# Stick-breaking attention on Trainium2: value sums on unsplit fp32 operands, two heads in the two column halves of TensorE

## The chip, the cores and the metric
One core of one Trainium2 chip runs the whole program. The metric is the device time in microseconds (us) of one execution. TensorE (PE) multiplies, VectorE (DVE), ScalarE (ACT) and GpSimd (POOL) work element by element, SyncE (SP) issues the transfers.

## What is computed
Two transformer-like blocks on one sequence of 1024 rows and 1024 channels, in fp32. The first block is a short-convolution layer and a stick-breaking attention layer with 16 heads of 64; the second has pooling, differential attention and a feed-forward part. The change is in the attention of the first block:

```
z = q @ k.T / sqrt(64);  mask = kpos < qpos
log_beta = log_sigmoid(z);  log_1m_beta = where(mask, log_beta - z, 0)
suffix = reverse_cumsum(log_1m_beta) - log_1m_beta
a = where(mask, exp(log_beta + suffix), 0);  o = a @ v
x = x + gate * ((o * silu(zgate)) @ w_out)
```

## The kernel before
TensorE's fast way takes operands of a rounded fp32 type (F32R). To keep fp32 accuracy, an operand is split into a high part, rounded by ScalarE, and a low part, the remainder, formed by VectorE in `low` (its instruction stands at L1420) or by GpSimd. A product is then two or three matmuls. A matmul whose operands are plain F32 needs no split; the trace lists two instructions for each.

**The kv stage** makes keys and values for eight pairs of heads (`kv_chunks`, 16 chunks of 48 matmuls). The values of a pair are evicted to VST, turned by TensorE, and written to VS by ScalarE (`values_hi`, high part) and VectorE (`values_lo`, low part). High and low values of a head lie beside each other, 64 and 64 columns, so that one weight load of 128 columns holds both. VS goes to DRAM (1024 KB a pair) and comes back later in bV.

**The attention stage** (`attention_b`) has one round j for each pair of heads; round 0 stands ahead of a loop, six rounds run in the loop, and round 7 (`fill=False`) behind it. A round has eight steps t, one for each block of 128 queries. What each engine does in a step t:

- TensorE: `scores(t)` for both heads (head h in row half h of PE, into PSUM pair 1+h), then `turn(t-1, h)`, which transposes the weights of the step before, in groups of up to four blocks that alternate between two PSUM banks, then, if t is even, `values(t-1, h)`, the sums over the values for the 256 queries of blocks t-2 and t-1. Between them `steps(n)` places n of the 96 matmuls of the next round's query and gate projection (`B_FILL` says how many in which place: a, c, d, e).
- ScalarE: `weigh(t, h)` (two sigmoids, L1135 and L1136) and, between the heads, `turned(t-1, h)`, the eviction of a transposed group to ATH (L1128); at even t also `lower`, which copies 64 rows of each head's value sums (L1146).
- VectorE: `left(t, h)`, the running product along the keys (a scan, L1601), and behind each head's scan `turned(t-1, h)`, which forms ATL = PSUM - ATH (L1420, semaphore b_atl); at even t `outputs`, which adds the other 64 rows (L1610).
- GpSimd: the product of beta and the running product (L1882), and at odd t `gated`, the multiplication with the gate (L1873).

All of it is an order written out by hand. A scan waits for the second sigmoid of its head; `scores(t+1)` waits until both scans of step t have read PSUM (`free[1+h]`); `turn(t-1, h)` waits for GpSimd's product and for the ATL of the group two back, whose bank it takes; `values(t-1, h)` waits for the last ATL of its head. For each key block it issues two matmuls of 256 columns (128 at the diagonal block), one on ATH and one on ATL, with 128 weight columns, the high and low values of that head. Its 128 output rows are two halves that still have to be added, which `lower` and `outputs` do. Groups and counts are kept by `pair_group`. At odd t no value sums are made.

## Time and profile before

| | us |
|---|---|
| time, median of 3 runs (3079.27 to 3080.32) | 3079.79 |
| profiled execution | 3079.05 |
| its span | 3077.3 |
| PE busy | 2841.6 (92%) |
| DVE busy | 1271.5 (41%) |
| ACT busy | 1128.6 (37%) |
| POOL busy | 716.3 (23%) |

The attention stage of the first block lies from 725 to 1200 us. Its rounds in the loop take 58.9 us each: the scores of t=1 begin at 1020.76 us in one round and at 1079.63 us in the next. Busy is time with an instruction under way; a matmul's end is modelled, so PE's issue is read from the starts of successive rows. A time of the timeline is in us from the span's start. In a row, the bracket behind it is the idle time of the engine before it and what ended it. "PEclk" is the granted clock of TensorE as a share of full speed.

### The profile page before, as it was taken

To read this page: it belongs to the slowest core of one execution; us is meant where nothing else is said; L and a number is where in the kernel's file an instruction comes from. 1 tells how busy PE (TensorE), PEld (TensorE's weight loads), DVE (VectorE), ACT (ScalarE), POOL (GpSimd) and SP (SyncE) were. 2 spreads that over 40 slices of the span, in tenths; PEclk is the share of its full clock that TensorE was granted. 3 is DMA by queue.
4 is the path that set the end of the run, shared out by engine and by line. 5 is a ranking of instruction groups with operands and counts; after the bars stand their busy time and mean duration, and the time that the engine had idled before them with its cause. 6 is when DMAs were issued, how large, how long until landed. Compare 5 with 4: busy or idle time off the path is not lost.

```text
span 3077.3 us, 38234 instructions
## 1 busy us (share of the span) xinstructions
PE 2841.6 (92%) x13672; PEld 2282.4 (74%) x13672; DVE 1271.5 (41%) x1817; ACT 1128.6 (37%) x1586; POOL 716.3 (23%) x387
## 2 busy tenths in 40 slices
PE   5999998998888888798999999998898999999999
PEld 3888886886777777677876766765686888888887
DVE  5544433116666666370014655657433312112121
ACT  3222213225666554333125666665312212111120
POOL 0222221223444443112221111110121222222222
PEclk8999999998999998999999999999898999999999
DMA  5333320552121122112331001011421111111112
GB/s 196 128 123 116 130 70 33 186 181 84 49 89 55 48 82 87 44 41 96 116 119 35 28 28 34 35 34 48 149 91 41 48 48 48 48 48 48 47 54 97
DMA packets 62571, 236.82 MB, mean 77 GB/s; under 512 B 6944, under 2 KB 7584, under 8 KB 59936
## 3 DMA queue, kind: packets, MB, share of 16 engines
q1 hardware_dynamic: 62496, 235.88, 22.3%
q8 instruction: 40, 0.66, 0.1%
q14 instruction: 35, 0.29, 0.0%
HBM read 191.81 MB, written 44.04 MB: 77 GB/s over the span
## 4 chain that ended last, share of the span: by engine, by line
PE 47%; issue 38%; DVE 7%; POOL 4%; ACT 3%; DMA 0%; POOLq 0%; DVEq 0%; ACTq 0%; SPq 0%
PE PS L558 37%; POOL WL L1854 3%; DVE bC L1601 2%; DVE ATL L1420 2%; PE PS L718 2%; PE PS L740 2%; PE PS L674 2%; ACT PS L1136 1%; PE PS L905 1%; PE PS L768 1%; PE PS L886 1%; PE PS L703 1%; PE PS L723 0%; DMA TMP<-mods 0%; ACT ATH L1310 0%
## 5 line engine op out<-in xcount | busy, mean ns | idle before, releaser
L1854 POOL TENSOR_TENSOR WL<-WR,WH 128x1024 fp32r<-128x1024 f32 x215 | 518.2, 2410 | 2071.6 <-ACT WH L1004 1939.2
L558 PE MATMUL PS<-HH,WH 128*128 128x512 f32 x2256 | 715.7, 399 | 85.0 <-issue 29.9
L558 PE MATMUL PS<-HL,WH 128*128 128x512 f32 x2256 | 704.1, 394 | 0.0
L558 PE MATMUL PS<-HH,WL 128*128 128x512 f32 x2256 | 702.7, 393 | 0.0
L558 PEld LDWEIGHTS PS<-HH,WH 128*128 128x128 f32 x2256 | 421.7, 191 | 187.5 <-issue 65.7
L558 PEld LDWEIGHTS PS<-HL,WH 128*128 128x128 f32 x2256 | 429.3, 190 | 91.5
L558 PEld LDWEIGHTS PS<-HH,WL 128*128 128x128 f32 x2256 | 428.8, 190 | 91.3
L1004 ACT ACTIVATE WH<-WR 128x1024 fp32r<-128x1024 f32 x214 | 225.9, 1056 | 642.3 <-PE PS L558 462.9
L558 PE MATMUL PS<-GH,WH 128*128 128x512 f32 x768 | 236.6, 389 | 1.5 <-DVE TMP L1824 1.5
L558 PE MATMUL PS<-GL,WH 128*128 128x512 f32 x768 | 236.5, 389 | 0.0
L558 PE MATMUL PS<-GH,WL 128*128 128x512 f32 x768 | 236.4, 389 | 0.0
L1882 POOL TENSOR_TENSOR bB<-bB,bC 128x256 f32<-128x256 f32 (+7 forms) x128 | 154.2, 1207 | 276.7 <-DVE bC L1601 275.6
L1601 DVE TENSOR_TENSOR_SCAN bC<-PS,EPSC 128x256 f32<-128x256 f32 (+7 forms) x128 | 172.8, 1350 | 96.7 <-ACT PS L1136 96.3
L558 PEld LDWEIGHTS PS<-GH,WH 128*128 128x128 f32 x768 | 144.0, 188 | 32.1 <-issue 1.9
L558 PEld LDWEIGHTS PS<-GH,WL 128*128 128x128 f32 x768 | 144.2, 188 | 30.0
L558 PEld LDWEIGHTS PS<-GL,WH 128*128 128x128 f32 x768 | 144.2, 188 | 29.9
L1420 DVE TENSOR_TENSOR ATL<-PS,ATH 128x512 fp32r<-128x512 f32 (+3 forms) x288 | 151.3, 544 | 32.0 <-ACT ATH L1310 25.9
L1846 DVE TENSOR_TENSOR X<-PS,X 128x1024 f32 x32 | 39.2, 1225 | 292.2 <-PE PS L558 292.2
L1837 DVE SCALAR_TENSOR_TENSOR TMP<-PS,TMP 128x1024 f32<-128x1024 f32 x32 | 39.2, 1224 | 207.6 <-ACT TMP L1399 207.6
L703 PE MATMUL PS<-IDF,bB 128*128 128x128 f32 x576 | 93.7, 291 | 28.1 <-DVE ATL L1420 28.0
L1399 ACT ACTIVATE TMP<-PS 128x1024 f32<-128x1024 f32 x32 | 32.9, 1029 | 233.2 <-PE PS L558 233.2
L1479 DVE CUSTOM_DVE_ANT_0 TMP<-TMP,TMP 128x1024 f32<-128x1024 f32 x48 | 59.8, 1246 | 132.8 <-DMA TMP<-mods 131.5
(226 smaller groups left out, 3579.8 us busy)
## 6 DMA issues: line engine op xcount, KB each, us to landing
WR<-wst SPq DMA_DIRECT2D x215, 512.0 KB, 3.5
TMP<-mods SPq DMA_DIRECT2D x48, 512.0 KB, 3.6
MRAW<-mods SPq DMA_DIRECT2D x16, 512.0 KB, 10.7
v_hl<-VS SPq DMA_DIRECT2D x8, 1024.0 KB, 6.3
bV<-v_hl SPq DMA_DIRECT2D x8, 1024.0 KB, 7.8
X<-xt SPq DMA_DIRECT2D x4, 1024.0 KB, 8.0
x_b<-X SPq DMA_DIRECT2D x8, 512.0 KB, 4.8
k_hi<-KSH SPq DMA_DIRECT2D x8, 512.0 KB, 5.0
```

The source lines that it names most:

```text
L558: last = pe.matmul(PS[:, dst0 + q:dst0 + q + HALF], l, rr[:, k * S + q:k * S + q + HALF], start=a, stop=z)
L674: last = pe.matmul(PS[:, OB + (2 * n + r) * P:OB + (2 * n + 2) * P], v[:, kb * P:(kb + 1) * P], a[:, (2 * kb + r) * P:(2 * kb + 2) * P], s ...
L703: last = pe.transpose(PS[:, base + n * P:base + (n + 1) * P], bB[t % 2][h][:, kb * P:(kb + 1) * P], IDF[:, :])
L718: pe.matmul(PS[:, base + c0:base + c0 + w], l[par][rows, q], rr[par][rows, c0:c0 + w], start=i == 0, stop=i == 2 and c0 + w < n)
L740: last = pe.matmul(PS[:, o + r * P:o + 2 * P], value_weights(V, kb, h), a[:, (2 * kb + r) * P:(2 * kb + 2) * P], start=i == 0 and a is ATH ...
L1004: act.activation(WH[slot][:, :], WR0[:, :], ACT.Identity).then_inc(w_hi, 1)
L1420: return dve.tensor_tensor(dst, value, high.bitcast(F32), ALU.subtract)
L1479: dve.tensor_tensor_reduce(out=weights, in0=weights, in1=CB, scale=1.0, scalar=0.0, op0=ALU.mult, op1=ALU.add, accum_out=dst).then_inc(mod ...
L1601: dve.tensor_tensor_scan(bC[h][:, S - n:S][:, ::-1], c, EPSC[:, 0:1].broadcast_to([P, n]), 1.0, ALU.mult, ALU.bypass).then_inc(free[1 + h], 1)
L1837: dve.scalar_tensor_tensor(out=T[2 + m], in0=PAIR[s], scalar=0.0, in1=T[m], op0=ALU.max, op1=ALU.mult).then_inc(free[s], 1)
L1854: pool.tensor_tensor(WL[slot][:, :], WR0[:, :], WH[slot][:, :].bitcast(F32), ALU.subtract).then_inc(w_lo, 1)
L1882: pool.tensor_tensor(b, b, bC[h][:, S - n + 1:S + 1], ALU.mult).then_inc(b_a, 1)
```

## The change
The values are no longer split: VS and bV hold S columns of F32, ScalarE alone writes VS, and the store and the load are 512 KB. The transposed weights are not split either: ScalarE copies the groups of head 0, VectorE those of head 1, each into its own F32 tile of a double-buffered bAT, each with its own semaphore. `values(t)` handles both heads together: for each key block one F32 matmul a head, with 64 weight columns, head 0 into PSUM partitions 0 to 63 and head 1 into 64 to 127, of the same columns; it waits for both heads' groups. Value sums alternate between two halves of their bank. Their 128 rows are whole, so `lower` and the additions go, and `outputs` multiplies them with the gate on VectorE, straight from PSUM, in place of `gated` on GpSimd. In the last round the output of t=1 is gated in step 4 rather than 2.

```diff
@@ layout and names
-        VS = place("VS", 2 * S, F32R, r)
+        VS = place("VS", S, F32, r)
...
-        bOT = place("bOT", 2 * P, F32, r)
...
-        bV = [place(f"bV{i}", 2 * S, F32R, r) for i in range(2)]
+        bV = [place(f"bV{i}", S, F32, r) for i in range(2)]
...
+        bAT = [[nc.alloc_sbuf_tensor_at(f"bAT{i}{h}", [P, 2 * S], F32, offset=XAT + 8 * S * (2 * i + h)) for h in range(2)]
+               for i in range(2)]
...
         def value_weights(V, kb, h):
-            return V[:, (2 * kb + h) * P:(2 * kb + h + 1) * P]
+            return V[:, kb * P + h * HD:kb * P + (h + 1) * HD]
+        def value_bank(t):
+            o = OB + (t // 2) % 2 * 2 * P
+            return o, o + 2 * P
@@ SyncE: one 512 KB store and one 512 KB load of values a pair of heads
-                sp.dma_start(row(v_hl, i), VS[:, :].bitcast(F32)).then_inc(st_v, 16)
+                sp.dma_start(row(v_t, i), VS[:, :]).then_inc(st_v, 16)
@@ TensorE, turn(t, h)
-                        before = pair_group(t, h, g) - 1
-                        if not (first and before <= 0):
-                            pe.wait_ge(b_atl, NB * j + before)
+                        t0, h0, g0 = pair_group_two_back(t, h, g)
+                        if not (first and t0 < 0):
+                            pe.wait_ge(b_at[h0], NG * j + (group_index(t0) + g0 + 1))
@@ TensorE, values
-                def values(t, h):
+                def values(t):
                     if t < 0 and first:
                         return
-                    if not (first and t < 2):
-                        pe.wait_ge(b_os, ST * j + (t - 1))
-                    pe.wait_ge(b_atl, NB * j + pair_group(t, h, len(GROUP_BLOCKS[t % ST])))
+                    if not (first and t == 1):
+                        pe.wait_ge(b_o, ST // 2 * j + (t - 1) // 2)
+                    for h in range(2):
+                        pe.wait_ge(b_at[h], NG * j + group_index(t + 1))
                     V, t = bV[par if t >= 0 else 1 - par], t % ST
-                    o = OB + 2 * h * P
+                    o, end = value_bank(t)
                     for i, kb in enumerate((0, t, *range(1, t))):
                         r = 1 if kb == t else 0
-                        for a in (ATH[h], ATL[h]):
-                            last = pe.matmul(PS[:, o + r * P:o + 2 * P], value_weights(V, kb, h),
-                                             a[:, (2 * kb + r) * P:(2 * kb + 2) * P],
-                                             start=i == 0 and a is ATH[h], stop=i == t and a is ATL[h])
+                        for h in range(2):
+                            last = pe.matmul(PS[h * HD:(h + 1) * HD, o + r * P:end], value_weights(V, kb, h),
+                                             bAT[t // 2 % 2][h][:, (2 * kb + r) * P:(2 * kb + 2) * P],
+                                             start=i == 0, stop=i == t)
                     last.then_inc(b_av, 1)
...
                     if t % 2 == 0:
-                        values(t - 1, 0)
                         steps(d)
-                        values(t - 1, 1)
+                        values(t - 1)
@@ ScalarE: values of the kv stage in one copy; turned takes head 0 alone; lower is gone
-                act.activation(value_part(0), PAIR[2].rearrange("p (a d) -> p a d", d=HD), ACT.Identity).then_inc(kv_vh, 1)
+                act.activation(VS[:, :], PAIR[2], ACT.Identity).then_inc(free[2], 1)
...
-                def turned(t, h):
+                def turned(t):
...
-                    if t % 2 == 0 and not (first and t < 2):
-                        act.wait_ge(b_av, ST * j + (t - 1 + h))
+                    if t % 2 == 0 and not (first and t < 4):
+                        act.wait_ge(b_av, ST // 2 * j + (t // 2 - 1))
...
-                        act.wait_ge(b_t, NB * j + (pair_group(t, h, g) + 1))
-                        act.activation(at_blocks(ATH[h], t % 2, bl[0], bl[-1] + 1),
-                                       turned_blocks(len(bl), turn_bank(t, h, g)), ACT.Identity).then_inc(b_ath, 1)
+                        act.wait_ge(b_t, NB * j + (pair_group(t, 0, g) + 1))
+                        act.activation(at_blocks(bAT[t // 2 % 2][0], t % 2, bl[0], bl[-1] + 1),
+                                       turned_blocks(len(bl), turn_bank(t, 0, g)), ACT.Identity).then_inc(b_at[0], 1)
@@ VectorE: values_lo is gone; turned copies head 1; outputs gates
-                        dve.wait_ge(b_ath, NB * j + (pair_group(t, h, g) + 1))
-                        b = (t % 2, bl[0], bl[-1] + 1)
-                        low(at_blocks(ATL[h], *b), turned_blocks(len(bl), turn_bank(t, h, g)),
-                            at_blocks(ATH[h], *b)).then_inc(b_atl, 1)
+                        dve.wait_ge(b_t, NB * j + (pair_group(t, 1, g) + 1))
+                        dve.tensor_copy(at_blocks(bAT[t // 2 % 2][1], t % 2, bl[0], bl[-1] + 1),
+                                        turned_blocks(len(bl), turn_bank(t, 1, g))).then_inc(b_at[1], 1)
...
+                def outputs(t):
...
+                    b = slice((t % ST - 1) * P, (t % ST + 1) * P)
+                    o, end = value_bank(t % ST)
+                    y = bZS[par if t >= 0 else 1 - par][:, b]
+                    if t == 1 or t == 5:
+                        dve.wait_ge(b_df, 4 * j + (1 if t == 1 else 2))
+                    dve.wait_ge(b_av, ST // 2 * j + (t + 1) // 2)
+                    dve.tensor_tensor(y, PS[:, o:end], y, ALU.mult).then_inc(b_o, 1)
...
                 for t in range(ST):
                     left(t, 0)
-                    turned(t - 1, 0)
                     left(t, 1)
-                    turned(t - 1, 1)
+                    turned(t - 1)
                     if t in halves:
                         evict(halves[t])
                     if not fill and t == ST - 1:
                         operand_lo("y", 0, bZS)
-                    if t % 2 == 0:
-                        outputs(t - 1, 0)
-                        outputs(t - 1, 1)
+                    if not fill and t == 4:
+                        outputs(1)
+                    if t % 2 == 0 and (fill or t != 2):
+                        outputs(t - 1)
@@ GpSimd: gated is gone
-                    if t % 2 == 1:
-                        gated(t - 2)
```

`pair_group_two_back(t, h, g)` gives the step, head and group that stand two places ahead in the order of groups. The staging tiles of the output projection move by one place, since bV is smaller.

## Rows read from the trace of the kernel before

**Rows 1.** Windows: length, busy us of PE, PEld, DVE, ACT, POOL; clock, DMA.
```profile
902.00:961.00 59.00, 52.28 (x355) 42.53 (x355) 37.79 (x52) 35.43 (x70) 26.64 (x22) 1.00 0.18 62
1138.00:1200.00 62.00, 46.82 (x292) 39.03 (x292) 39.23 (x50) 35.63 (x67) 26.82 (x20) 0.83 0.16 57
```

**Rows 2.** Waits in two middle rounds: us in total, times, longest us.
```profile
PE PS L718 <- DVE bC L1601: 5.3, 8, 1.2
PE PS L703 <- DVE ATL L1420: 5.0, 4, 1.3
PE PS L740 <- DVE ATL L1420: 3.0, 6, 0.7
```

**Rows 3.** Groups by line, two middle rounds: count, busy us, mean ns.
```profile
L1420 DVE TENSOR_TENSOR ATL<-PS,ATH 128x512 fp32r<-128x512 f32 (+3 forms) x48 | 24.5, 539 | 1.1 <-ACT ATH L1128 0.9
L1610 DVE TENSOR_TENSOR bOT<-PS,bOT 64x256 f32<-64x256 f32 x16 | 6.8, 422 | 17.9 <-ACT bOT L1146 17.7
```

**Rows 4.** Timeline, steps 4, 5, 7: last sigmoid (L1136), second scan (L1601): start, us.
```profile
1038.12 0.72 ACT L1136 ACTIVATE PS<-PS 128x640 f32<-128x640 f32 x1
1039.16 1.48 DVE L1601 TENSOR_TENSOR_SCAN bC<-PS,EPSC 128x640 f32<-128x640 f32 x1
1040.56 0.67 DVE L1420 TENSOR_TENSOR ATL<-PS,ATH 128x512 fp32r<-128x512 f32 x1
...
1046.69 0.84 ACT L1136 ACTIVATE PS<-PS 128x768 f32<-128x768 f32 x1
1047.94 1.75 DVE L1601 TENSOR_TENSOR_SCAN bC<-PS,EPSC 128x768 f32<-128x768 f32 x1
...
1067.03 1.05 ACT L1136 ACTIVATE PS<-PS 128x1024 f32<-128x1024 f32 x1
1068.64 2.28 DVE L1601 TENSOR_TENSOR_SCAN bC<-PS,EPSC 128x1024 f32<-128x1024 f32 x1
```

**Rows 5.** Timeline, steps 4, 6, 0, TensorE: value sums and what follows.
```profile
1041.28 0.39 PE L740 MATMUL PS<-ATH,bV 128*128 128x256 f32 x1 [0.72 <-DVE ATL L1420]
1042.40 0.50 PE L718 MATMUL PS<-bKH,bQH 64*128 64x512 f32 x2
...
1059.03 0.39 PE L740 MATMUL PS<-ATH,bV 128*128 128x256 f32 x1 [0.42 <-DVE ATL L1420]
1060.54 0.40 PE L768 MATMUL PS<-HH,WH 128*128 128x512 f32 x1
...
1075.53 0.28 PE L740 MATMUL PS<-ATH,bV 128*128 128x256 f32 x1
1079.63 0.39 PE L718 MATMUL PS<-bKH,bQH 64*128 64x256 f32 x2
```

**Rows 6.** Timeline, TensorE: matmuls on unsplit fp32 operands, start and us.
```profile
1608.15 1.02 PE L849 MATMUL PS<-dSQ,dBD 128*128 128x512 f32 x2
1608.58 0.59 PE L849 MATMUL PS<-dSQ,dBD 128*128 128x512 f32 x1
```

**Rows 7.** Timeline, TensorE: scores of step 3, heads in two row halves.
```profile
1029.54 0.40 PE L718 MATMUL PS<-bKL,bQH 64*128 64x512 f32 x2
1029.77 0.40 PE L718 MATMUL PS<-bKH,bQL 64*128 64x512 f32 x2
```

**Rows 8.** Timeline: end of the kv stage.
```profile
689.52 1.23 DVE L1420 TENSOR_TENSOR VS<-PS,VS 128x1024 fp32r<-128x1024 f32 x1 [13.17 <-ACT VS L1092]
692.03 1.15 ACT L1017 ACTIVATE HH<-TMP,MOD 128x1024 fp32r<-128x1024 f32 x1 [2.54 <-DVE TMP L1413]
700.73 0.79 PE L558 MATMUL PS<-HH,WH 128*128 128x512 f32 x1 [4.13 <-DVE KSL L1420]
```

**Rows 9.** Timeline: last round, second scan, value sums, what follows.
```profile
1186.86 2.28 DVE L1601 TENSOR_TENSOR_SCAN bC<-PS,EPSC 128x1024 f32<-128x1024 f32 x1
1194.63 0.56 PE L740 MATMUL PS<-ATH,bV 128*128 128x256 f32 x1
1199.73 0.40 PE L558 MATMUL PS<-HH,WH 128*128 128x512 f32 x1
```

More of the change, by code:

```diff
@@ L145 @@
 NB = 2 * NG
+PAIR_GROUPS = [(t, h, g) for t in range(ST) for h in range(2) for g in range(len(GROUP_BLOCKS[t]))]
 def pair_group(t, h, g=0):
@@ L151, in pair_group, with pair_group_two_back @@
     return NB * ((t - t0) // ST) + 2 * (GROUPS[t0] - len(GROUP_BLOCKS[t0])) + h * len(GROUP_BLOCKS[t0]) + g
+def pair_group_two_back(t, h, g):
+    n = pair_group(t, h, g) - 2
+    t0, h0, g0 = PAIR_GROUPS[n % NB]
+    return t0 + ST * (n // NB), h0, g0
 def group_index(s):
@@ L233, in block_kernel @@
                       for i, n in enumerate(places)]
-               for name, at, places in (("y", (B_KV + 127) // 128 * 128, (0, 2, 4, 5)), ("ab", slots, (0, 2, 4, 6)))}
+               for name, at, places in (("y", (B_KV + 127) // 128 * 128, (0, 2, 4, 6)), ("ab", slots, (0, 2, 4, 6)))}
         r = [ATT0]
@@ L258, in block_kernel @@
         k_hi, k_lo = (scratch(n) for n in ("k_hi", "k_lo"))
-        v_hl = nc.dram_tensor("v_hl", [KT, P, 2 * S], F32, kind="Internal").ap()
-        y_b, m_p, g_a, y_d, x_b, x_d = (scratch(n) for n in ("y_b", "m_p", "g_a", "y_d", "x_b", "x_d"))
+        v_t, y_b, m_p, g_a, y_d, x_b, x_d = (scratch(n) for n in ("v_t", "y_b", "m_p", "g_a", "y_d", "x_b", "x_d"))
         def at_blocks(t, r, lo, hi):
@@ L340, in block_kernel @@
         b_df = sem("b_df")
-        b_oc = sem("b_oc")
-        b_os = sem("b_os")
         b_a = sem("b_a")
         b_t = sem("b_t")
-        b_ath = sem("b_ath")
-        b_atl = sem("b_atl")
+        b_at = [sem(f"b_at{h}") for h in range(2)]
         b_av = sem("b_av")
@@ L440, in load_kv @@
             def load_kv(j, par):
-                for src, dst in ((k_hi, bKH), (k_lo, bKL), (v_hl, bV)):
+                for src, dst in ((k_hi, bKH), (k_lo, bKL)):
                     sp.dma_start(dst[par][:, :].bitcast(F32), row(src, j)).then_inc(b_ld, 16)
+                sp.dma_start(bV[par][:, :], row(v_t, j)).then_inc(b_ld, 16)
             with sp.Fori(0, KT - 1) as i:
@@ L800, in attention_b @@
                 turn(ST - 1, 1)
-                values(ST - 1, 0)
-                values(ST - 1, 1)
+                values(ST - 1)
                 pe.wait_ge(b_df, 4 * KT - 2)
-                pe.wait_ge(b_atl, NB * KT)
+                pe.wait_ge(b_at[1], NG * KT)
                 two_chunks(C_BOUT, (0, 1), (0, 1), USED["bout"], (f_lo, FILL["y"]))
@@ L1136, in weigh @@
                     act.activation(src, src, ACT.Sigmoid, scale=-HD ** -0.5).then_inc(b_c, 1)
-                def lower(t, h):
-                    if t < 0 and first:
-                        return
-                    act.wait_ge(b_av, ST * j + (t + 1))
-                    if not (first and t < 2):
-                        act.wait_ge(b_o, ST // 2 * j + (t - 1) // 2)
-                    rows, other = slice(h * HD, (h + 1) * HD), slice((1 - h) * HD, (2 - h) * HD)
-                    act.activation(bOT[rows, :], PS[other, OB + 2 * h * P:OB + 2 * (h + 1) * P], ACT.Identity).then_inc(b_oc, 1)
                 def evict(i):
@@ L1554, in _ @@
             fill_lo("kv", 2, lambda k: col(COEF, KT + k), 3 * KT)
-            def values_lo(i):
-                dve.wait_ge(kv_vh, i + 1)
-                low(value_part(1), PAIR[2].rearrange("p (a d) -> p a d", d=HD), value_part(0)).then_inc(free[2], 1)
             def keys_lo(i):
@@ L1563, in _ @@
             with dve.Fori(0, KT - 1) as i:
-                values_lo(i)
                 keys_lo(i)
-            values_lo(KT - 1)
             fill_lo("qz", 2, lambda k: col(COEF, 2 * KT + k), 5 * KT, before=lambda k: keys_lo(KT - 1) if k == 4 else None)
@@ L1583, in attention_b, with turned @@
             def attention_b(j, par, fill=True, first=False):
-                def turned(t, h):
+                def turned(t):
                     if t < 0 and first:
                         return
+                    if t % 2 == 0 and not (first and t < 4):
+                        dve.wait_ge(b_av, ST // 2 * j + (t // 2 - 1))
                     for g in range(len(GROUP_BLOCKS[t % ST])):
                         bl = blocks_of(t % ST, g)
-                        dve.wait_ge(b_ath, NB * j + (pair_group(t, h, g) + 1))
-                        b = (t % 2, bl[0], bl[-1] + 1)
-                        low(at_blocks(ATL[h], *b), turned_blocks(len(bl), turn_bank(t, h, g)),
-                            at_blocks(ATH[h], *b)).then_inc(b_atl, 1)
+                        dve.wait_ge(b_t, NB * j + (pair_group(t, 1, g) + 1))
+                        dve.tensor_copy(at_blocks(bAT[t // 2 % 2][1], t % 2, bl[0], bl[-1] + 1),
+                                        turned_blocks(len(bl), turn_bank(t, 1, g))).then_inc(b_at[1], 1)
                 def left(t, h):
@@ L1628, in attention_b @@
                     left(t, 0)
[L1629 removed]
                     left(t, 1)
[L1631 removed]
+                    turned(t - 1)
                     if t in halves:
@@ L1888, in attention_b @@
                         split_w(2 * j + (C_QZ + 3), 1)
-                if not fill:
-                    gated(ST - 1)
             attention_b(0, 0, first=True)
```

33 lines of the change are left out of this document (3 added, 30 removed).

## Prediction, made before the changed kernel was run

> **What bounds the kernel now.** I read the page first (PE busy for 92% of the span), then the windows of the attention stage, its waits, and the timeline of one round of the loop, because an average over the span says nothing of a stage that takes 475 us of 3077. In the middle of that stage PE is busy for 52.3 of 59.0 us and VectorE for 37.8; in the last round PE is busy for 46.8 of 62 us and its clock falls to 0.83 of full speed [rows 1]. So a round is nearly full of matmuls, and what is left are short waits. In two rounds PE waits 5.3 us for the scans, 5.0 us to transpose into a bank that the low part has not released, and 3.0 us for the low part ahead of the value sums [rows 2]: 6.65 us a round. The last two kinds, 4.0 us a round, end at the instructions that the change takes away. The reader should see that this is the most that the waits on ATL are worth, and that it isn't what will be gained, since behind each of them the next scan may be late anyway.
>
> **The scans come earlier.** VectorE forms 24 low parts a round, 12.2 us [rows 3]; 12 of them become copies, 12 go. The ones that go are those of head 0, and they stand between the two scans of a step. In step 4 the second sigmoid ends at 1038.12 + 0.72 = 1038.84 and the scan that needs it starts at 1039.16; in step 5 it is 1047.53 and 1047.94, in step 7 1068.08 and 1068.64 [rows 4]. So the second scan is late by 0.32, 0.41 and 0.56 us, and I take 0.3, 0.4 and 0.5 us as what it gains; steps 1 and 3 get 0.3 like step 4, step 2 half of that, step 6 0.45, between its neighbours (estimates from those rows). No more than that, because the second sigmoid on ScalarE doesn't move: between the two heads ScalarE still evicts head 0. In steps 1, 3, 5 and 7 the next scores wait for this scan: 0.3 + 0.3 + 0.4 + 0.5 = 1.5 us a round gained. The waits of the transposes for their bank go as well (ScalarE alone now releases head 0's), but PE then arrives earlier at the same scan, so I give them nothing.
>
> **The value sums.** This is the part that no row of before shows as it will be. A matmul on unsplit fp32 operands is two instructions, and with 512 columns one starts 0.43 us after the other (1608.15 and 1608.58) [rows 6], twice the 0.23 us of a pair of split ones in the scores [rows 7]. For 256 columns I halve it: 0.215 us each. A key block needs two for each head, four in all. A round has t+1 key blocks for t = 1, 3, 5, 7, of which the diagonal one is half as wide: 1.5, 3.5, 5.5 and 7.5, together 18 blocks. If the heads run one behind the other, a block takes 0.87 us. If the column halves work at the same time, it takes 0.435 us: then head 0's second instruction runs beside head 1's first, and head 1's second beside head 0's first of the next block. The nearest row is the one of the scores, where the two heads lie in the two row halves of PE: two matmuls of 512 columns have one start, and the next two follow after 0.23 us (1029.54, 1029.77) [rows 7], the time of one. I therefore take 0.435 us and keep 0.87 us as the other end. The sums are then 0.65, 1.52, 2.39 and 3.26 us long; I add 0.15 us for going over to another shape of PE and back (bounds 0 and 0.5, an estimate from the start-to-start times of 0.1 to 0.2 us between unlike matmuls of these rows).
>
> The Trainium skill (TensorE: Matmul & The Clock Gate, Part 3, Measured speedup vs the span model) gives 2.38 times for three column tiles, so it would have the halves run together. No run shown here has a column tile.
>
> Against this stands a new wait. Before, head 0's sums started at once and only head 1's waited for the end of VectorE's work. Now both wait for head 1's copy, which stands behind the second scan; behind the waiting sums in PE's queue stand the scores of the next step, for which ScalarE waits. So in steps 2, 4 and 6 the old time from the start of head 1's sums is what the new sums replace. Step 4: they started at 1041.28, the scores at 1042.40, 1.12 us [rows 5]; the copy comes 0.3 us earlier and takes what the low part took (0.67 us [rows 4], same source, same columns; below it the gain would be at most a few tenths). New minus old: -0.3 + 1.52 + 0.15 - 1.12 = +0.25 us. Step 6: -0.45 + 2.39 + 0.15 - 1.51 = +0.58 us (1059.03 to 1060.54 [rows 5]). Step 2, with 1.5 blocks and an old time of some 0.55 us by the two others: -0.15 + 0.80 - 0.55 = +0.10 us. In step 0 nothing is waited for: PE's own steps end later than the copy. The old sums of t=7 took 1075.53 to 1079.63 less one projection matmul of 0.23 us, 3.87 us [rows 5]; the new ones 3.26 + 0.15 = 3.41, -0.46 us.
>
> Round: -1.5 + 0.10 + 0.25 + 0.58 - 0.46 = -1.03 us. Seven rounds: -7.2 us.
>
> **Outputs.** The 16 additions of two rounds are 6.8 us of VectorE [rows 3]; one multiplication of 256 columns in place of two takes half. ScalarE's copies and GpSimd's gating go. They stand behind the value sums, beside the next scores, so they cost nothing; without that cover it would be one instruction of 0.42 us [rows 3] for each of four steps. Only in the last round does one matter: step 4 has to gate t=1 before the sums of t=3 may start, +0.45 us.
>
> **The kv stage.** The stores and loads of values are half as large and hidden on both sides. In the steady part PE is full and nothing is gained. At its end VectorE forms the last low values from 689.52 for 1.23 us, and only then starts the next operands; ScalarE starts on them at 692.03 and had waited 2.54 us; PE then stands still for 4.13 us, until 700.73 [rows 8]. With `values_lo` gone, this chain starts up to 2.5 us earlier, but the last keys still need their chunk. I take 2 us (bounds 0 and 2.5).
>
> **The last round.** It has the scans' gain and the even steps' loss of the others, -1.5 + 0.93 = -0.57 us, and +0.45 us for the late gating. Its final sums took 1194.63 to 1199.73, 5.1 us, at a clock that starts low [rows 1, 9]. The new ones are 3.26 us at 2.4 GHz and twice that at 1.2 GHz; I take 4.6 us, -0.5 us. Together -0.6 us (bounds -3 and +2).
>
> **Sum.** -7.2 - 2.0 - 0.6 = -9.8 us. The profiled execution took 3079.05 us (span 3077.3), so 3069.3 us; the median of the runs stands 0.74 us above it: 3070 us.
>
> **Rivals.**
> 1. *The column halves don't overlap.* For it: the four instructions of a block come as two of head 0, then two of head 1, in order, and these are of another kind than the scores. Then 18 x 0.435 = 7.8 us more a round, 63 us over eight, none of it hidden, because the scores of the next step stand behind: 3070 + 63 = 3133 us, slower. It decides as soon as a block takes over 0.5 us: the 9.8 us are used up at 1.2 us a round, 0.07 us a block. In the Trainium skill (TensorE: Matmul & The Clock Gate, Part 3, The mechanism) weight loads overlap running matmuls "only when row_grp differs"; two column halves have the same rows, so by that sentence head 1's weights wait for head 0's matmul, and the case is this one. That page's measured column tiles speak against it. In this trace weight loads (PEld, busy for 42.5 us) lie beside matmuls (PE, 52.3 us) in the same 59 us [rows 1], on full-height weights.
> 2. *Half of it.* Only the inner two of a block's four run together, 0.65 us a block: 18 x 0.22 = 3.9 us a round more, 31 us: 3101 us.
> 3. *The wait for both heads eats it.* The halves overlap, but a switch costs 0.3 us rather than 0.15 (+0.6 a round) and the scans gain half of what I took (+0.5 or so): the rounds change by nothing, the kv stage's 2 us are left, 3078 us. For it: three of the four sums get longer already in my working.
>
> **Chances.** My forecast 50%, its own range 3062 to 3076 us (the switch, the copy's length and the last round). Rival 1 28%, rival 2 10%, rival 3 12%. A measurement tells this kernel from no change at about 0.2%, 6 us. Faster by more: the forecast less its upper tail, 48%. Within: that tail and rival 3, 14%. Slower: rivals 1 and 2, 38%. The range has to reach rival 1 to leave out no more than 2 in 10: 3061 to 3134 us.
>
> **What would show it.** Right: value matmuls of the two heads in pairs with one start, or a block every 0.43 to 0.45 us; the second scan within 0.05 us of the sigmoid's end; a round of 57.9 us; the first projection matmul after the kv stage some 2 us earlier. Wrong: four starts 0.215 us apart in a block, and a round of 65 us or more; or a gap ahead of the value sums of step 6 that is longer than the 3 us which the missing work of head 0 leaves there. A slower VectorE copy than 0.67 us would also make it wrong, in steps 2, 4 and 6.

## The result, and the profile after

The change made the kernel slower: 3088.2 us (median of 11 runs, 3083.3 to 3089.6) against 3080.1 us for the kernel before in the same session (11 runs, 3078.2 to 3088.1). The ratio is 1.002, its 95% interval 1.0011 to 1.0029. The forecast was 3070 us. A second set of runs of the same kernel (`a1_again`, below) gave 1.0021. The loss is small, and the spans of two traces of one kernel differ by 1.5 to 2.1 us, so its places are counted on two traces of each kernel.

The profiled execution took 3086.9 us. From its page: the span, then busy time of each engine with its share and its instructions.

```profile
span 3085.1 us, 37583 instructions
PE 2836.7 (92%) x13672; PEld 2259.0 (73%) x13672; DVE 1212.3 (39%) x1681; ACT 1064.0 (34%) x1426; POOL 695.2 (23%) x355
```

The page alone would mislead: PE and VectorE have both less to do than before, and the span is 7.8 us longer. The line of the value sums in the same page (busy us, mean ns of one, idle time ahead and what ended it) has the reason in its last figures: 43.8 us of standing still ahead of them, ended by VectorE's copy.

```profile
L747 PE MATMUL PS<-bAT,bV 128*64 128x256 f32 (+1 forms) x640 | 79.8, 401 | 45.5 <-DVE bAT L1574 43.8
```

The waits of two middle rounds (total us, times, longest), in place of [rows 2]:

```profile
PE PS L747 <- DVE bAT L1574: 10.5, 6, 3.0
PE PS L724 <- DVE bC L1584: 5.4, 8, 1.5
```

The wait for scans is the old one (5.4 against 5.3 us). Transposes no longer wait for a bank (5.0 us gone), but the value sums wait 10.5 us in place of 3.0. Since each line of waits names only who came last, the sum of all, 15.9 against 13.3 us, already points to the even steps.

The timeline of step 6 (start us, us, engine, line; idle before and its releaser), in place of the middle of [rows 5]:

```profile
1054.16 0.40 PE L775 MATMUL PS<-HH,WL 128*128 128x512 f32 x1
...
1054.49 2.02 DVE L1584 TENSOR_TENSOR_SCAN bC<-PS,EPSC 128x896 f32<-128x896 f32 x1 [0.38 <-ACT PS L1141]
...
1056.43 1.00 DVE L1574 COPY bAT<-PS 128x512 f32<-128x512 f32 x2
...
1057.57 3.81 PE L747 MATMUL PS<-bAT,bV 128*64 128x256 f32 x24 [3.01 <-DVE bAT L1574]
...
1061.31 0.80 PE L775 MATMUL PS<-HH,WH 128*128 128x512 f32 x1
...
1062.85 0.50 PE L724 MATMUL PS<-bKH,bQH 64*128 64x512 f32 x2
```

PE ends its projections at 1054.56, the second scan runs until 1056.51, then come the copies of head 1, and only at 1057.57 may the sums of both heads start. From the first start of the 24 instructions to that of the next one it is 3.74 us, where the prediction had 2.39 + 0.15 = 2.54. The windows around them say why (length; busy PE, PEld, DVE, ACT, POOL; granted clock; DMA):

```profile
1054.00:1057.50 3.50, 0.56 (x3) 0.12 (x2) 3.12 (x5) 1.05 (x2) 2.69 (x2) 1.00 0.34 136
1057.50:1061.40 3.90, 3.83 (x25) 2.44 (x25) 0.52 (x1) 0.00 (x0) 0.86 (x1) 0.67 0.00 0
1061.40:1062.80 1.40, 1.40 (x4) 0.93 (x4) 0.42 (x1) 0.00 (x0) 0.00 (x0) 0.71 0.00 0
```

In this pause the clock still reads full. It falls to its lower level, 1.2 GHz, while the sums run: the mean is 0.67 over the sums and 0.71 over the projections behind. In other rounds it is at the lower level already in the last 0.5 to 0.8 us of the pause, as in round 3 (first line below, clock 0.50). Either way nearly all of the price lies behind the pause and not in the line of the wait. In the trace of before no middle round has such a fall; here five of six have one, in `a1_again` six of six. Round 1 is the one without; its same 24 instructions take 2.53 us from start to start (818.47 to 821.00), as the prediction had them:

```profile
935.95:936.70 0.75, 0.00 (x0) 0.00 (x0) 0.75 (x3) 0.00 (x0) 0.75 (x1) 0.50 0.00 0
```

```profile
818.47 2.60 PE L747 MATMUL PS<-bAT,bV 128*64 128x256 f32 x24 [3.01 <-DVE bAT L1574]
821.00 0.50 PE L775 MATMUL PS<-HH,WH 128*128 128x512 f32 x1
```

The 3 us are not only the time that head 0's sums leave empty (12 instructions, 1.6 us in the kernel before). PE also waited 1.32 us for a bank in that step and 0.42 us for the low part. The first of these waits is gone, so PE comes to the sums earlier and stands there instead. This is its row in step 6 of before:

```profile
1055.86 0.87 PE L703 MATMUL PS<-IDF,bB 128*128 128x128 f32 x6 [1.32 <-DVE ATL L1420]
```

**The steps.** From the first score of one step to the first of the next, a middle round (us; t0 is step 0 to 1, and so on):

```
          t0    t1    t2    t3    t4    t5    t6            t7    round
before    8.66  3.43  5.01  5.14  8.06  7.34  11.81         9.43  58.88
after     8.30  3.00  5.18  4.95  8.42  6.96  12.60         8.91  58.31  (round 1, no fall)
          "     "     "     "     "     "     13.93..15.45  "     59.7..61.1 (rounds 2 to 6)
```

**The whole.** Three parts, in each kernel's two traces (before and `b1_before_again`; after and `a1_again`):

```
                            before           after            mean difference
until the first scores      721.8, 720.9     717.0, 718.6     -3.5
attention stage             477.8, 477.7     483.1, 485.8     +6.7
the rest, code unchanged    1877.7, 1880.8   1885.0, 1882.2   +4.4
```

The attention stage is the change's own. So is a part of the first row: the first scores of one and the same code come at 716.5 to 721.2 us in eight traces, so its -3.5 holds chance too, and the kv stage is measured more closely below. The third row is the second block and what follows, where no instruction of the loops was touched; I come back to it too.

### The profile page after: what moved, and what is told of

Read it like the earlier page. It is cut to its first block, busy times and chain, and to the rows that moved or that the text cites. A ratio compares the mean times of both kernels' runs of the same rounds, so it can differ in the third digit from the quotient of the medians.

```text
span 3085.1 us, 37583 instructions
## 1 busy us (share of the span) xinstructions
PE 2836.7 (92%) x13672; PEld 2259.0 (73%) x13672; DVE 1212.3 (39%) x1681; ACT 1064.0 (34%) x1426; POOL 695.2 (23%) x355
## 4 chain that ended last, share of the span: by engine, by line
issue 57%; PE 26%; POOL 6%; ACT 5%; DVE 5%; POOLq 0%; ACTq 0%; DMA 0%; DVEq 0%; SPq 0%
PE PS L564 15%; POOL WL L1838 6%; PE PS L747 2%; PE PS L724 2%; DVE bC L1584 2%; PE PS L680 2%; ACT PS L1141 1%; ACT bB L1140 1%; PE PS L910 1%; ACT bAT L1133 1%; PE PS L775 1%; PE PS L891 1%; DVE ATL L1408 1%; DVE bAT L1574 1%; PE PS L709 1%
## 5 line engine op out<-in xcount | busy, mean ns | idle before, releaser
L1140 ACT ACTIVATE bB<-PS 128x256 f32<-128x256 f32 (+7 forms) x128 | 83.7, 654 | 231.0 <-PE PS L729 231.0
L747 PE MATMUL PS<-bAT,bV 128*64 128x256 f32 (+1 forms) x640 | 79.8, 401 | 45.5 <-DVE bAT L1574 43.8
```

The source lines that it names most:

```text
L747: last = pe.matmul(PS[h * HD:(h + 1) * HD, o + r * P:end], value_weights(V, kb, h), bAT[t // 2 % 2][h][:, (2 * kb + r) * P:(2 * kb + 2) * ...
L1140: act.activation(bB[t % 2][h][:, 0:n], src, ACT.Sigmoid, scale=HD ** -0.5)
```

## Experiments

Two theories on the slower attention stage. Theory A: the wait for both heads in step 6, 3 us long, drops the clock behind it, and that costs more than all the scans' gains. Theory B: the column halves are not as good as they look (a part of them runs in turn), and the clock follows from the longer stage. What I expected of a run of the changed kernel as it is comes first, as the yardstick.

**a1_again**, the changed kernel unaltered.

> The changed kernel once more, unaltered, for a second trace. Theory 1 (the clock): between the copy of head 1 and the last projection matmul of step 6 PE stands still for 3.0 us in every round, and in most rounds the granted clock falls to 0.5 right behind it; step 6 (scores to scores) then takes 13.9 to 15.5 us against 12.6 us in a round without the fall. Expected again: 12.6 us where the clock stays, 14 us or more where it falls, in at least four of the six middle rounds; the time 1.002 of before. Theory 2 (the value sums of step 6 are slow in themselves, since two instructions a head on column halves don't overlap when there are many): 24 instructions take 3.8 us in every round, fallen clock or not. Theory 3 (chance in unchanged code): the 7 us that the first trace of after has behind the attention stage, in code that is the same in both, come at another size or place in this trace.

3086.07 us (3082.8 to 3088.7, 11 runs), ratio 1.0021 [1.0012, 1.003]. The loss is repeatable; every middle round's step 6 took 13.9 to 14.2 us.

**e1_fill** keeps PE busy through the pause with matmuls that nobody reads:

```diff
+                    if fill and t == 5:
+                        o, end = value_bank(t)
+                        for _ in range(24):
+                            pe.matmul(PS[:, o:end], HH[:, 0:P], HH[:, 0:2 * P], start=True, stop=True)
                     for h in range(2):
                         pe.wait_ge(b_at[h], NG * j + group_index(t + 1))
```

> 24 matmuls of 256 columns without use are put ahead of the value sums of step 6 (into the PSUM half that the sums overwrite), where PE stood still for 3.0 us: 24 x 0.118 = 2.8 us. All else is as in the changed kernel. Theory 1 (the pause lets the clock fall): the clock stays at 1.00 through step 6, step 6 takes 12.6 to 12.8 us in every round, some 1.6 us less in each of the rounds in which it fell, 8 to 12 us less than the changed kernel in all: a little faster than before, about 0.999. Theory 2 (the sums are slow themselves): step 6 stays at 14 us or more, and the time doesn't fall.

3084.16 us (3083.1 to 3088.5), ratio 1.0017 [1.0007, 1.0026]. The timeline in step 6:

```profile
872.80 3.04 PE L743 MATMUL PS<-HH 128*128 128x256 f32 x24
...
876.04 2.17 PE L751 MATMUL PS<-bAT,bV 128*64 128x256 f32 x20 [0.20 <-DVE bAT L1578]
```

Step 6 is 12.6 us in all six middle rounds, and none of them has a fall in it: theory A's mechanism is shown, since nothing but PE's idleness was taken away. But the median is only 2 us below `a1_again` (4 below the changed kernel's first set), where six falls cost some 9; I had expected 8 to 12 us less. The waits of rounds 1 to 6 show a new kind, here with `a1_again` in the second fence:

```profile
PE PS L724 <- DVE bC L1588: 16.1, 24, 1.5
PE PS L751 <- DVE bAT L1578: 14.1, 16, 1.5
PE PS L724 <- issue: 4.0, 2, 2.2
```

```profile
PE PS L747 <- DVE bAT L1574: 34.4, 19, 3.1
PE PS L724 <- DVE bC L1584: 16.2, 24, 1.5
```

Twice PE stands still for some 2 us at the start of a pass of the loop, while nothing that it waits for is late (`issue`), and the clock falls behind that: step 0 takes 11.62 and 13.13 us there in place of 8.30, which gives back 8.2 us. A filler of PE instructions is a poor cure here.

**e8_fill_half**: the same with 12 instead of 24.

> As e1, with 12 matmuls without use instead of 24: PE's pause ahead of the value sums of step 6 is shortened from 3.0 to some 1.6 us, not filled. In e1 no clock fell in step 6, but PE twice stood still for 1.8 and 2.2 us inside the scores at the start of a pass of the loop, waiting for nothing that the profile shows, with a fall behind it. Theory (the length of the pause decides, and the 24 extra instructions brought e1's two other pauses): every middle round takes 58.3 us, step 6 12.6 us, without those pauses; the attention stage takes 474 to 476 us against 481.3 in e1 and 483 to 486 in the changed kernel; the time 3077 to 3080 us, 0.999 to 1.000 of before. Rival (a pause of 1.6 us lets the clock fall as well): step 6 takes 14 us again in most rounds, 3086 us.

3082.69 us (3075.7 to 3086.3), ratio 1.0006 [0.9996, 1.0015]. The pause in step 6 is now at most 1.6 us and no middle step 6 has a fall (12.6 us each), so in this place a pause half as long is harmless; it does not have to be filled whole. The other half of what I expected failed: with half of the added instructions the `issue` pauses remained, the attention stage took 482.5 us and not 474 to 476, and the time lies above the 3077 to 3080 us. The pauses and the falls behind them show in steps 0 of 11.65 and 10.91 us and steps 7 of 10.44 and 10.05, and in this row at the start of a pass:

```profile
893.31 0.33 PE L724 MATMUL PS<-bKH,bQH 64*128 64x128 f32 x2 [2.36 <-issue]
```

**e2_copy_first** takes the wait itself away. In even steps VectorE copies head 1's transposes between its two scans, not behind them:

```diff
                     left(t, 0)
+                    if t % 2 == 0:
+                        turned(t - 1)
                     left(t, 1)
-                    turned(t - 1)
+                    if t % 2:
+                        turned(t - 1)
```

> At even t VectorE copies head 1's transposed group between the two scans instead of behind both; nothing else is moved. Theory 1 (what the changed kernel pays is the wait of both heads' sums for a copy that stands behind the second scan, and the clock that falls in it): in step 6 the copy ends some 2 us earlier and the sums start at once or within 0.5 us, no clock falls there, step 6 takes 10 to 10.5 us instead of 12.6 or 14.2; in step 4 the sums start 1.5 us earlier; the second scan is later by 0.3 to 0.6 us, which shows in the waits of the scores. A round of 55 to 57 us instead of 59.9, 0.992 to 0.996 of before. Rival (the scan that is put off costs as much, since everything hangs on the two scans of a step): a round of 58 us or more, 0.998 or above.

3034.82 us (3033.5 to 3039.7, 4 runs), ratio 0.9859 [0.9843, 0.9875]: 45 us faster than the kernel before and 51 faster than the changed one beside it, more than the 0.992 to 0.996 that I expected. Step 6:

```profile
965.69 2.02 DVE L1584 TENSOR_TENSOR_SCAN bC<-PS,EPSC 128x896 f32<-128x896 f32 x1 [2.74 <-ACT PS L1141]
...
967.63 1.00 DVE L1574 COPY bAT<-PS 128x512 f32<-128x512 f32 x2
968.54 2.01 DVE L1584 TENSOR_TENSOR_SCAN bC<-PS,EPSC 128x896 f32<-128x896 f32 x1
968.77 2.60 PE L747 MATMUL PS<-bAT,bV 128*64 128x256 f32 x24 [0.66 <-DVE bAT L1574]
```

The copies now run while the second sigmoid is formed, PE waits 0.66 us and the same 24 instructions take 2.60 us, the length at the full clock. The second scan starts at once behind the copies, 0.45 us later than it did (2.85 us behind the first scan, 2.40 in the changed kernel), and PE's wait for scans stays what it was. The waits of two middle rounds, where 10.5 us stood in the changed kernel:

```profile
PE PS L724 <- DVE bC L1584: 5.5, 8, 1.5
PE PS L747 <- DVE bAT L1574: 1.3, 2, 0.7
```

A round takes 53.57 us with 4.37, 6.87 and 10.22 us in steps 2, 4 and 6: 4.75 us less than the changed kernel's round without a fall. That is about the 4.6 us by which the waits shrank ((10.5 - 1.3) / 2). So the position of the copy was worth 4.7 us a round by itself, and the falls 1.3 to 2.9 us on top. The attention stage went from 483.1 to 437.4 us.

**e3_heads_in_turn** is for theory B. The loop over heads goes outside that over key blocks, so the two column halves should get nothing to do at one time:

```diff
-                    for i, kb in enumerate((0, t, *range(1, t))):
-                        r = 1 if kb == t else 0
-                        for h in range(2):
+                    for h in range(2):
+                        for i, kb in enumerate((0, t, *range(1, t))):
+                            r = 1 if kb == t else 0
```

> The same value matmuls, but all key blocks of head 0 and then all of head 1, so that never two instructions on different column halves are next to each other but once. Theory (the column halves run together only where the two heads' instructions are neighbours in the queue): a block costs 0.87 instead of 0.435 us, the 32 instructions of t=7 take 6.5 instead of 3.4 us, a round is 7.8 us longer: 3088 + 62 = 3150 us, 1.022 of before. Rival (the halves don't need to alternate, or the gain comes from narrower weight loads): no change, 3088 us.

3123.97 us (3117.6 to 3124.4, 4 runs), ratio 1.0139 [1.0123, 1.0156]; the round 64.5 us. The sums of t=7 in this kernel and, second, in the changed one:

```profile
1102.49 5.86 PE L747 MATMUL PS<-bAT,bV 128*64 128x256 f32 x32
```

```profile
1076.65 3.46 PE L747 MATMUL PS<-bAT,bV 128*64 128x256 f32 x32
...
1080.04 0.39 PE L724 MATMUL PS<-bKH,bQH 64*128 64x256 f32 x2
```

Theory B falls: with heads alternating, 32 instructions start within 3.39 us, the 3.26 of the prediction plus 0.13. Grouped by head they take 5.86, not the 6.45 that they would in a row (28 of 0.215 us and four of half the columns), and a round is 4.6 us longer (62.90 against 58.31 where neither has a fall in step 6, 64.55 against 59.9 where both have), not the 7.8 us of rival 1. The last section shows why.

**e4_before_copy_first** asks whether e2 needs the change at all: the same reordering in the kernel before (head 1's low part between the scans).

```diff
                     turned(t - 1, 0)
+                    if t % 2 == 0:
+                        turned(t - 1, 1)
                     left(t, 1)
-                    turned(t - 1, 1)
+                    if t % 2:
+                        turned(t - 1, 1)
```

> The kernel before, with split operands, but at even t VectorE forms head 1's low part ahead of the second scan, as the copy in e2. It tells whether e2's 45 us belong to the new order alone or need the change. Theory (they need it: in the old kernel the low part waits for head 1's high part, which ScalarE writes behind the second pair of sigmoids, and the transposition of head 1 waits for a low part of head 0): the second scan is put off by 1 us or more in each even step, a round stays at 58 us or more, 0.995 to 1.01 of before. Rival (the order alone does it): a round of 55 to 56 us, 0.992 or less.

3073.11 us (3070.5 to 3077.9, 10 runs), ratio 0.9978 [0.9969, 0.9988]: 7 to 8 us, not 45. A middle round takes 57.9 us in place of 58.9: steps 2 and 4 gain 0.4 and 0.9 us, step 6 loses 0.35:

```profile
933.36 1.02 DVE L1420 TENSOR_TENSOR ATL<-PS,ATH 128x512 fp32r<-128x512 f32 x2 [1.05 <-ACT ATH L1128]
...
934.30 2.01 DVE L1601 TENSOR_TENSOR_SCAN bC<-PS,EPSC 128x896 f32<-128x896 f32 x1
```

VectorE waits 1.05 us there for ScalarE's high part of head 1, with the second scan queued behind. A low part needs the high part first, a plain copy doesn't: the same reordering is worth 7 to 8 us in the old kernel and 51 in the new one.

**e5_copy_first_always**: the copy between the scans in every step, odd ones too (`turned(t - 1)` ahead of `left(t, 1)` without a condition).

> The changed kernel with the copy of head 1 between the two scans in every step, odd ones too. At odd t no value sums wait for the copy, but the scores of the next step wait for the second scan. Theory: at odd t the second scan, and with it the next scores, are later by what the copy and the wait for its transposition cost, 0.3 to 0.9 us in each of four steps: 1.5 to 3 us a round more than e2's 53.57 us, 3046 to 3058 us. Rival (the copy fits between the scans unseen, since the second scan waits for ScalarE's sigmoid anyway): 53.6 us a round as e2.

3072.04 us (3063.2 to 3075.3, 6 runs), ratio 0.997 [0.9957, 0.9983]: 37 us worse than e2, and above the 3046 to 3058 us of my theory. In step 7:

```profile
881.96 1.15 DVE L1574 COPY bAT<-PS 128x512 f32<-128x512 f32 x2 [1.20 <-PE PS L709]
883.03 2.28 DVE L1584 TENSOR_TENSOR_SCAN bC<-PS,EPSC 128x1024 f32<-128x1024 f32 x1
...
885.36 0.33 PE L724 MATMUL PS<-bKH,bQH 64*128 64x128 f32 x2 [2.65 <-DVE bC L1584]
```

In an odd step the transposes come late and nobody is in a hurry for the copy, but the second scan is what the next scores wait for. The copy waits 1.20 us, the scan behind it too, PE 2.65 us, and step 7 takes 10.73 us instead of 8.91. Without falls the odd steps and step 0 together cost 2.4 us a round more than in e2, within the 1.5 to 3 that I expected. What I left out is again the clock: in every middle round it falls, in turn in step 6 (11.6 to 11.7 us in place of 10.2) and in step 0 (10.8 to 10.9 in place of 8.0), and a round takes 57.4 to 58.9 us. The same instruction in the same place is right in even steps and wrong in odd ones.

**e6_low_again** gives back the 1.2 us of VectorE that the kv stage lost: one useless subtraction of 1024 columns where the low values stood.

```diff
+            def values_again(i):
+                dve.wait_ge(free[2], i + (USED["kv"][2] + 1))
+                dve.tensor_tensor(VX[:, :], kt(X, 0), kt(X, 1), ALU.subtract)
...
```

> The changed kernel, with one VectorE instruction of 1024 columns without use in the place of each low part of the values in the kv stage. Theory (the end of the kv stage gained 2 us of VectorE's chain, and another 1.6 us because PE's pause there, 2.4 instead of 4.1 us, no longer lets the clock fall): the first scores start at 721 to 722 us instead of 717.0 to 718.6, PE's pause ahead of the projection is some 4 us again, and the granted clock falls behind it; the time rises by 3 to 4 us over the changed kernel, 1.003 of before. Rival (the gain comes from the smaller transfers or from ScalarE's plain copy): no change, 717 to 718.6 us.

3085.68 us (3082.9 to 3087.5, 10 runs), ratio 1.0015 [1.0006, 1.0025]: no difference from the changed kernel by time, where I had expected 3 to 4 us more. The trace shows the place. The first projection matmul after the kv stage and the first scores, here and then in the changed kernel:

```profile
699.66 0.73 PE L565 MATMUL PS<-HH,WH 128*128 128x512 f32 x2 [4.14 <-DVE KSL L1409]
...
719.92 0.33 PE L725 MATMUL PS<-bKH,bQH 64*128 64x128 f32 x2 [2.05 <-DVE bQL L1409]
```

```profile
697.54 0.73 PE L564 MATMUL PS<-HH,WH 128*128 128x512 f32 x2 [2.38 <-DVE KSL L1408]
...
717.04 0.33 PE L724 MATMUL PS<-bKH,bQH 64*128 64x128 f32 x2 [2.05 <-DVE bQL L1408]
```

The pause is the old one again, 4.14 us ([rows 8]: 4.13); in the eight other traces of the new code it is 2.37 or 2.38. From the start of the pause to the first scores it takes 24.4 us here and 21.9 to 22.6 in those eight. So the shorter pause comes from the removed low values. The times of the rows themselves show less: the scores come 2.9 us later than in the trace beside it, but `e8_fill_half`, whose kv stage is that of the changed kernel, has them at 719.46 us.

**e7_gate_early**: e2, with the gating of t=1 in the last round ahead of step 4's scans, because in e2 it is late:

```profile
1116.81 3.03 PE L747 MATMUL PS<-bAT,bV 128*64 128x256 f32 x16 [2.03 <-DVE bZS L1597]
```

```diff
+                    if not fill and t == 4:
+                        outputs(1)
                     left(t, 0)
...
```

> As e2 (copy of head 1 between the scans at even t), and in the last round the gating of t=1, which stood behind the copy and the second scan of step 4, ahead of the first scan of that step. In e2's trace the value sums of t=3 wait 2.0 us for it there and then run at a fallen clock: step 4 of the last round takes 10.9 us against 6.87 us in the others. Theory (that wait and the fall behind it are all that sets this step apart): step 4 of the last round takes 7 to 7.5 us, 3.5 to 4 us less in all, 3031 us, 0.984 to 0.985 of before. Rival (the last round has fewer projection matmuls between, so PE stands still there anyway): step 4 stays above 9 us, no change.

3033.67 us (3030.1 to 3038.7, 4 runs), ratio 0.9849 [0.9831, 0.9868]. Step 4 of the last round takes 6.69 us instead of 10.91, with a wait of 0.67:

```profile
1116.78 1.74 PE L747 MATMUL PS<-bAT,bV 128*64 128x256 f32 x16 [0.67 <-DVE bAT L1574]
```

The attention stage is 6.7 us shorter in its trace (430.7 from 437.4), 4.2 of them in this step, but the first scores came 3.9 us later there. The medians differ by 1 us, less than the spread of either, so the two aren't told apart by time. Both beat both kernels.

**b1_before_again**, the kernel before in one more look.

> The kernel before, unaltered, for a second trace of it. From the last value sum to the end all kernels run the same instructions; this stretch took 1877.7 us in the trace of before, 1885.0 and 1882.2 in two of the changed kernel, 1883.0, 1879.6 and 1883.2 in three experiments. Theory 1 (which of the pauses in unchanged code meet a fallen clock differs from run to run): 1880 to 1885 us here too. Theory 2 (the change does something to the code behind it, such as the moved staging tiles): 1877 to 1878 us again. Rounds of the attention stage as before, 58.87 us, no fallen clock in them, in either case.

3081.17 us. Its first scores and attention stage are within 0.9 and 0.1 us of the first trace, but its unchanged rest is 3.2 us longer. In that rest the matrix multiplications of the second block show it (windows of `before`, `b1_before_again` and `after`, from the same instruction to the same):

```profile
1607.00:2170.00 563.00, 507.74 (x2619) 377.39 (x2620) 331.48 (x821) 349.44 (x551) 76.83 (x32) 0.96 0.10 34
```

```profile
1606.00:2172.00 566.00, 510.39 (x2618) 380.40 (x2619) 331.11 (x820) 349.23 (x551) 76.59 (x32) 0.95 0.10 34
```

```profile
1610.00:2178.00 568.00, 511.04 (x2618) 380.67 (x2619) 331.33 (x820) 349.86 (x551) 77.03 (x32) 0.95 0.10 34
```

The same instructions, busy for 2.7 to 3.3 us more on PE: clock falls on other waits, some 48 us at the lower level in the first trace, 54 in the second, 58 in the third. So part of the +4.4 us is what one trace differs from the next. Over all runs the unchanged rest is 1877.7 to 1880.8 us in the three traces on the old kernel's code and 1879.6 to 1885.0 in the nine on the new one's (means 1879.7 and 1882.5). Whether those 2.8 us belong to the change, by where the loops lie or in which phase they start, stays open.

## Why the prediction was wrong, step by step

**Overlap of the column halves (rival 1): right.** 0.215 us a pair of instructions, 3.39 us for t=7 against 3.26 + 0.15 predicted. The bound I was least sure of, and gave 38% to, held to 0.02 us. In the Trainium skill (TensorE: Matmul & The Clock Gate, Part 3, Measured speedup vs the span model) it is the measured table that this trace agrees with, here at 2 column tiles and fp32. By the sentence of The mechanism in the same part, that weights load beside a matmul only in another row group, rival 1 would have been the case; this trace doesn't agree, since both heads use all rows and their matmuls still run beside each other.

**The scans in odd steps: right.** t1 -0.43 (-0.3), t3 -0.20 (-0.3), t5 -0.38 (-0.4), t7 -0.52 (-0.5); together -1.53 against -1.5. The second scan of step 4 starts 0.04 us behind the sigmoid's end, of the 0.32 of before:

```profile
1037.05 0.72 ACT L1141 ACTIVATE PS<-PS 128x640 f32<-128x640 f32 x1
...
1037.81 1.49 DVE L1584 TENSOR_TENSOR_SCAN bC<-PS,EPSC 128x640 f32<-128x640 f32 x1 [0.21 <-ACT PS L1141]
```

**The even steps: small errors, and the one that decided.** t0 -0.36 (-0.46), t2 +0.17 (+0.10), t4 +0.35 (+0.25). Step 6 was to cost +0.58: without a fall it cost +0.79, with one +2.1 to +3.6. The sums themselves (2.53 us without a fall) and the copy (0.67 us for 512 columns) are as predicted. The failed step is the sentence "So in steps 2, 4 and 6 the old time from the start of head 1's sums is what the new sums replace" and the term -0.45 + 2.39 + 0.15 - 1.51: it priced the matmuls at the full clock. It took the start of the sums as fixed by the scan and asked only how long they are, not what PE does until then. Before, head 0's sums lay in that time, and the wait for a bank ahead of them, to whose removal I gave nothing; both gone, 3.01 us were left. I had written that length down ("longer than the 3 us which the missing work of head 0 leaves there") as harmless. Yet the last round's sums were priced at half clock behind a wait, so the mechanism was in my hands. The Trainium skill warns of it (TensorE: Matmul & The Clock Gate, HAM oscillation), there for waits on DMA: matmul groups between waits that each start at the low clock, pass after pass; this trace agrees in five passes of six, with 3.81 us for the 24 instructions against 2.60 in e2, and the rest on the projections behind.

**Ledger of the rounds.** Predicted -7.2 us for rounds 0 to 6. In the profiled execution round 0 came to +0.9 (55.70 from 54.80; its step 4, in which the clock falls in both kernels, took 9.55 from 8.62), the six middle rounds to +5.35: -0.57 x 6 = -3.4 without falls, +8.8 by five falls. Without falls I was off by 0.46 us a round, 0.2 of it in step 6, the rest in tenths over the other steps.

The profiled execution ends 17.6 us above the forecast (+7.8 against -9.8). Rounds 0 to 6 make 13.4 of them. The kv stage and the last round came out 2.7 and 0.4 us better. The code behind the attention stage, for which the sum has no term, makes 7.3 (4.4 as the mean of two pairs). So about half of the whole miss is the falls in step 6, and a part, behind the stage, has no shown cause.

**The last round: right within its bounds.** -1.0 us against -0.6 (68.66 from 69.66); in the second pair of traces +0.3 (69.73 from 69.43), with falls in steps 4 and 6 of `a1_again`. The sums took 5.02 us where I had 4.6; the late gating of +0.45 and step 4's +0.25 together measured +0.34 (8.63 from 8.29).

**The kv stage: right in kind, low in size.** 2.0 predicted; the pause shrank by 1.75 us (4.13 to 2.38). The first scores come 4.7 us earlier (3.5 as the mean of two pairs), but their place varies by over 4 us among traces of one code, mostly ahead of the pause. From the start of the pause to the first scores it is steadier: 25.0 to 25.2 us in three traces on the old code; in eight on the new one 21.9 where the clock doesn't fall behind the pause and 22.4 to 22.6 where it does. So the stage gained 2.4 to 3.3 us: 1.75 in the pause, and the rest goes with the clock behind it. Behind the old pause the clock fell in all three traces, behind the new one in four of eight (`a1_again`, e3, e7, e8). The windows of `before`, `after` and `a1_again` around the pause:

```profile
700.00:708.00 8.00, 7.28 (x21) 5.80 (x22) 7.93 (x7) 2.34 (x3) 1.76 (x1) 0.64 0.59 194
```

```profile
697.00:705.00 8.00, 6.87 (x29) 5.43 (x30) 7.93 (x6) 3.52 (x4) 2.39 (x1) 1.00 0.52 168
```

```profile
698.00:706.00 8.00, 7.63 (x27) 6.16 (x28) 7.93 (x6) 3.35 (x3) 2.38 (x1) 0.79 0.53 176
```

**The rivals.** Rival 3, the wait for both heads, named the right place but neither its size nor its sign: it ended at 3078 us because it, too, knew only durations at one clock. No rival ended between 3078 and 3101 us, where the result is.

## What to carry to other kernels

When work leaves an engine, look at what it leaves in front of the next wait: a pause of TensorE that grew to 3 us cost not only itself but, in most passes, half the clock behind it, and a term of a few tenths turned into one of 2 to 3.6 us a pass. And when a consumer now waits for both halves of something, move the last producer's short instruction ahead of the long one in its queue, but only where the long one isn't itself the next thing waited for; here the change lost 8 us, and with that one move it gained 45.

## What was not expected of the hardware

- **Matmuls of one column half start ahead of earlier ones of the other.** In e3 all 16 instructions of head 0 stand ahead of head 1's 16 in the program. In the quarter of a microsecond from 1105.30 to 1105.56 seven are under way; each is at most 0.43 us long and starts in one half are 0.215 us apart, so one half alone would show three or four:

```profile
1104.90 1.02 PE L747 MATMUL PS<-bAT,bV 128*64 128x256 f32 x7
```

  The shape tells whose they are: head 0's two instructions of 128 columns are its third and fourth and stand at 1102.95 and 1103.06, yet at 1105.49 one of 128 columns starts, ahead of head 0's last at 1105.54, so it is head 1's. This is the row (instructions under way at 1105.74):

```profile
1105.49 0.49 PE L747 MATMUL PS<-bAT,bV 128*64 128x128 f32 x3
```

  Head 1's first four instructions start beside head 0's 13th to 16th. Two of the four are of half the columns; together they are 0.65 us, which accounts for the 0.6 us by which 5.86 falls short of 6.45, and for t=1, whose 8 instructions cost nothing extra in that order (step 2 takes 5.18 us in both). The Trainium skill (TensorE: Matmul & The Clock Gate, Part 3, The mechanism) has matmuls start and end strictly in program order; across column halves this trace doesn't agree.
- **A pause's length alone doesn't settle whether the clock falls behind it.** Behind the 3.0 us of step 6 it fell in 15 of 18 middle rounds (five, six and four of six in the changed kernel's two traces and e6), behind the 4.1 us at the end of the old kv stage in all traces. Behind the 2.37 us of the new kv stage, the same instructions every time, it fell in four traces of eight. Behind the 1.6 us of e8's step 6 it never fell, but behind the 1.84 us ahead of e5's step 6 it did in three rounds of six, and behind a wait of 1.2 us in one round of e4.
- **More TensorE instructions in the loop's body brought pauses of 1.3 to 2.4 us in the first step of some passes,** in which nothing waits for another engine: 2 of over 1 us in e1's middle rounds with 24 added, 3 of over 1 us in e8's with 12. No middle round of the changed kernel has one. What fetches or feeds them wasn't measured.
